# Dealing the routed token rows over the slot columns: ranks of an expert over eight groups of four, half of the experts backwards

## The reference

```python
group_p = softmax(xf @ w_group_router)            # 8 groups
g_w, g_idx = top_k(group_p, 1)
e_logits = (xf @ w_expert_router).reshape(N, 8, 8)
in_group = take_along_axis(e_logits, g_idx)       # the 8 experts of the group
e_w, e_idx = top_k(softmax(in_group), 2)          # two of them
gate = g_w * (e_w / sum(e_w))
expert = g_idx * 8 + e_idx
...                                               # per expert e, for its tokens:
a, b = split(x @ w_up[e], 2);  y = (silu(a) * b) @ w_down[e]
```

## Time and profile before

| | |
|---|---|
| median of 3 runs | 1333.13 us (1330.25 to 1333.38) |
| profiled execution, its own time | 1332.49 us |
| its span | 1330.7 us |
| mean granted clock of TensorE | 0.939 |
| routing, from its first constant to the first pair's up product | 629.2 to 670.3 us |
| pairs, first up product to the end of the last | 670.3 to 1191.2 us |
| busy share of the span | TensorE 85%, VectorE 47%, ScalarE 24%, GpSimd 18% |

### The profile page before, as it was taken

How to read it: one execution, slowest core, us unless ns; L and a number is a source line. 1 busy time by engine, 2 the same in 40 slices (tenths; PEclk the granted TensorE clock), 3 DMA queues, 4 the chain that set the end, 5 groups by cost and what they waited for, 6 DMA issues and landing times. The chain is left out here.

```text
span 1330.7 us, 16742 instructions
## 1 busy us (share of the span) xinstructions
PE 1125.5 (85%) x6261; PEld 733.2 (55%) x6262; DVE 626.4 (47%) x926; ACT 322.8 (24%) x693; POOL 242.6 (18%) x346
## 2 busy tenths in 40 slices
PE   6999899998788876998988888788878777872996
PEld 5888788876767765887432333333333322322885
DVE  5699999984778765232711111111111111125674
ACT  5212211116555534222311111100000000022332
POOL 4000100003676640001111110111111111101120
PEclk9999999999899997998989998998899988895999
DMA  6111111100000106121999999999999999967331
GB/s 209 32 48 33 47 49 48 48 16 1 1 2 2 65 1 214 64 95 47 415 393 427 424 424 413 423 404 399 409 413 406 412 401 401 408 267 270 133 127 64
DMA packets 70170, 281.30 MB, mean 211 GB/s; under 512 B 12570, under 2 KB 38363, under 8 KB 53467
## 3 DMA queue, kind: packets, MB, share of 16 engines
q1 hardware_dynamic: 57120, 258.53, 49.3%
q0 software_dynamic: 9376, 16.80, 3.3%
q10 hardware_dynamic: 3610, 5.11, 1.0%
HBM read 268.08 MB, written 29.62 MB: 224 GB/s over the span
## 5 line engine op out<-in xcount | busy, mean ns | idle before, releaser
L2582 PE MATMUL ps_u<-wup,xgT 128*64 128x512 f32 x1024 | 260.1, 666 | 72.3 <-DMA wup<-in_w_up_dram 71.5
L2582 PEld LDWEIGHTS ps_u<-wup,xgT 128*64 128x64 f32 x1024 | 87.0, 153 | 241.8 <-issue 240.8
L2449 DVE TENSOR_TENSOR hb<-sil,ps_u 128x256 f32<-128x256 f32 x32 | 13.5, 421 | 330.5 <-ACT sil L2343 330.5
L94 PE MATMUL ps_b<-n_hi,wh 128*128 128x512 f32 x384 | 157.7, 411 | 0.6 <-DVE wl L431 0.6
L94 PE MATMUL ps_b<-n_lo,wh 128*128 128x512 f32 x384 | 152.0, 396 | 0.0
L94 PE MATMUL ps_b<-n_hi,wl 128*128 128x512 f32 x384 | 151.8, 395 | 0.0
L2343 ACT ACTIVATE sil<-ps_u 128x256 f32<-128x256 f32 x32 | 12.3, 385 | 312.3 <-PE ps_u L2582 312.3
L94 PE MATMUL ps_y<-wg_hi,hx 128*128 128x512 f32 x256 | 83.4, 403 | 2.5 <-DVE hx L2524 2.5
L94 PEld LDWEIGHTS ps_b<-n_hi,wh 128*128 128x128 f32 x384 | 73.2, 191 | 16.5 <-issue 2.5
L94 PEld LDWEIGHTS ps_b<-n_hi,wl 128*128 128x128 f32 x384 | 73.1, 190 | 16.4
L94 PEld LDWEIGHTS ps_b<-n_lo,wh 128*128 128x128 f32 x384 | 73.3, 191 | 15.0 <-issue 1.0
(11 more groups left out here) (372 smaller groups left out, 1841.8 us busy)
## 6 DMA issues: line engine op xcount, KB each, us to landing
wup<-in_w_up_dram SPq DMA_DIRECT2D x64, 2048.0 KB, 16.7
zT<-in_w_down_dram SPq DMA_DIRECT2D x32, 1024.0 KB, 18.0
convT<-in_w_down_dram SPq DMA_DIRECT2D x32, 1024.0 KB, 17.3
wraw<-in_w_in_dram SPq DMA_DIRECT2D x24, 512.0 KB, 4.3
convT<-y_rows SPq DMA_DIRECT2D x16, 512.0 KB, 4.7
qkvT<-in_x_dram SPq DMA_DIRECT2D x8, 512.0 KB, 8.6
qkvT<-in_w_out_dram SPq DMA_DIRECT2D x8, 512.0 KB, 5.3
xr<-in_x_dram SPq DMA_DIRECT2D x8, 512.0 KB, 3.4
```

Of the source, the lines that this page charges most:

```text
L94: ins = nc.tensor.matmul(ps, lhs[a], rhs[b], start=first and k == 0, stop=last and k == 2)
L2449: nc.vector.tensor_tensor(hb[k][rows], sil[k][rows], ps_u[k][rows, FE:2 * FE], ALU.mult).then_inc(s_h, 1)
L2582: last = nc.tensor.matmul(ps_u[k][HC[c], :], xgT[k][:, j, HC[c]], wup[k][c][:, j, :], start=j == 0, stop=j == NJ - 1)
```

## The change

It has three parts. `iP` becomes one pattern over the 128 partitions: partition 32a + 4b + c (a 0 to 3, b 0 to 7, c 0 to 3) carries the slot value 32a + 8c + b. Consecutive ranks of an expert therefore go to partitions 4 apart, over eight groups of four partitions, and the upper expert now counts up from slot 64. Second, the experts whose place in their group (0 to 7) is 4 or more are filled backwards: `slot` becomes 63 - `slot`. For that the place in the group, `i1` and `i2` before, is kept in one tile `in`, and three instructions of VectorE are added: one that makes `back` (-2 for the experts concerned, else 0) and two that apply it. Third, `iP` takes one instruction of GpSimd in place of two, so the waits for s_iota count one less. Experts p and p + 32 have the same place in their groups, so both of a pair run the same way. Loops, buffers, waits and transfers of the pairs' stage are the same.

```diff
@@ constants and tiles
-t1 = {... "m1", "i1", "m2", "i2", "ex", ...}
-t2 = {n: ... for n in ("ev", "rank", ...)}
+t1 = {... "m1", "m2", "ex", ...}
+t2 = {n: ... for n in ("in", "back", "ev", "rank", ...)}
+            HS = P // 4
@@ vector
-                dve.wait_ge(s_iota, 10)
+                dve.wait_ge(s_iota, 9)
-                first(t8["ing"][:], t1["m1"][:], t8["e1"], t8["c1"], t1["i1"], t8["o1"])
+                first(t8["ing"][:], t1["m1"][:], t8["e1"], t8["c1"], t2["in"][:, :, 0:1], t8["o1"])
-                first(t8["d2"][:], t1["m2"][:], t8["e2"], t8["c2"], t1["i2"], t8["oh"])
+                first(t8["d2"][:], t1["m2"][:], t8["e2"], t8["c2"], t2["in"][:, :, 1:2], t8["oh"])
...
                 tt(ohs[:], oh[:, :, 0, :], oh[:, :, 1, :], ALU.add, "ohs")
+                then(nc.vector.tensor_scalar(t2["back"][:], t2["in"][:], -100.0 + 3.5, -2.0, ALU.is_ge, ALU.mult))
...
                 tt(t2["pair"][:], t2["c"][:], t2["ep"][:], ALU.add)
+                then(nc.vector.scalar_tensor_tensor(t2["b"][:], t2["slot"][:], -0.5 * (C - 1), t2["back"][:], ALU.add, ALU.mult))
+                tt(t2["slot"][:], t2["slot"][:], t2["b"][:], ALU.add)
                 tt(t2["a"][:], t2["up"][:], t2["mn"][:], ALU.mult)
                 tt(t2["slot"][:], t2["slot"][:], t2["a"][:], ALU.add)
@@ gpsimd
-                iota(iP[:, 0:C], [[1, C]], 0, 0)
-                iota(iP[:, C:P], [[-1, C]], P - 1, 0)
+                iota(iP, [[HS, P // HS], [1, 8], [8, HS // 8]], 0, 0)
...
-                pool.wait_ge(s_iota, 9)
+                pool.wait_ge(s_iota, 8)
@@ tensor
-                pe.wait_ge(s_iota, 10)
+                pe.wait_ge(s_iota, 9)
```

More of the change, by code:

```diff
@@ L1811, in hybrid_block_kernel @@
             t8 = {n: sb("r8_" + n, W8, ctx=c6) for n in ("gd", "ge", "eq", "ca", "oh", "ing", "d", "e1", "c1", "o1", "d2", "e2", "c2")}
-            t1 = {n: sb("r1_" + n, [P, NT, 1], ctx=c6) for n in ("gm", "gs", "gw", "gi", "m1", "i1", "m2", "i2", "ex", "dn", "rc")}
-            t2 = {n: sb("r2_" + n, [P, NT, 2], ctx=c6) for n in ("ev", "rank", "m", "slot", "ovk", "pk", "a", "b", "c", "up", "ep", "pair", "mp", "mn")}
+            t1 = {n: sb("r1_" + n, [P, NT, 1], ctx=c6) for n in ("gm", "gs", "gw", "gi", "m1", "m2", "ex", "dn", "rc")}
+            t2 = {n: sb("r2_" + n, [P, NT, 2], ctx=c6) for n in ("in", "back", "ev", "rank", "m", "slot", "ovk", "pk", "a", "b", "c", "up", "ep", "pair", "mp", "mn")}
             big = sb("r_big", [P, NT, NG, 8], ctx=c6)
@@ L1887, in _ @@
                 at["m2"] = done
-                first(t8["d2"][:], t1["m2"][:], t8["e2"], t8["c2"], t1["i2"], t8["oh"])
-                for k, i_k in enumerate(("i1", "i2")):
-                    then(nc.vector.scalar_tensor_tensor(t2["ev"][:, :, k:k + 1], t1["gi"][:], 8.0, t1[i_k][:], ALU.mult, ALU.add))
+                first(t8["d2"][:], t1["m2"][:], t8["e2"], t8["c2"], t2["in"][:, :, 1:2], t8["oh"])
+                for k in range(2):
+                    then(nc.vector.scalar_tensor_tensor(t2["ev"][:, :, k:k + 1], t1["gi"][:], 8.0, t2["in"][:, :, k:k + 1], ALU.mult, ALU.add))
                 then(nc.vector.tensor_scalar(t2["ev"][:], t2["ev"][:], 900.0, None, ALU.add))
@@ L1958, in iota @@
                 def iota(t, pattern, base, mult):
-                    nc.gpsimd.iota(t, pattern, base=base, channel_multiplier=mult, allow_small_or_imprecise_dtypes=True).then_inc(s_iota, 1)
-                iota(i8[:], [[1, 8]], 0, 0)
-                iota(i64[:], [[1, NE]], 0, 0)
-                iota(iP[:, 0:C], [[1, C]], 0, 0)
-                iota(iP[:, C:P], [[-1, C]], P - 1, 0)
-                iota(iN[:], [[1, NIP]], 0, 0)
-                iota(val[:], [[P, NT], [T, 2]], 1, 1)
+                    nc.gpsimd.iota(t[:], pattern, base=base, channel_multiplier=mult, allow_small_or_imprecise_dtypes=True).then_inc(s_iota, 1)
+                iota(i8, [[1, 8]], 0, 0)
+                iota(i64, [[1, NE]], 0, 0)
+                iota(iP, [[HS, P // HS], [1, 8], [8, HS // 8]], 0, 0)
+                iota(iN, [[1, NIP]], 0, 0)
+                iota(val, [[P, NT], [T, 2]], 1, 1)
                 nc.gpsimd.memset(on16[:], 1.0).then_inc(s_iota, 1)
```

## The result

The changed kernel takes 1312.8 us (median of four runs, 1312.5 to 1314.1) against 1332.0 us (four runs of the kernel before). The ratio is 0.9858, with a 95% interval of 0.9841 to 0.9875: 19.2 us faster, where 17.5 were forecast. The forecast of 1315.5 us is 2.7 us too high and its range of 1310 to 1322 holds the result. Measured again beside the experiments on one chip, it was 1314.0 against 1334.1, ratio 0.9853 (0.9836 to 0.9870). The profiled execution took 1312.5 us, span 1310.8.

A forecast was written before the change was run, and what follows sets the result against it. The prediction took the most heavily loaded DMA engine to set the pairs' pace. Rows -18.0 us and routing +0.5 gave -17.5 from the profiled 1332.5, so 1315.0; adjusted to the runs' median, 1315.5 us was forecast, range 1310 to 1322.

The forecast's parts named there:

- split A: Weight and row transfers: each DMA engine moves four neighbouring partitions and the four 32 further on, within one half.
- the working of the prediction: Pairs' stage, 28 gaps: 14.84 us a pair for an engine's weights plus 0.155 us per row of the heaviest engine.
- Split C: Rival, row transfers: groups of four partitions dealt round all 16 engines, without running ahead; 9.9 us more, 1343.5; chance 0.03.
- The rows: -18.0 us: Pairs' stage: the heaviest engine's counted rows fall from 374 to 258, at 0.155 us each, 18.0 us less.
- Running ahead: Pairs' stage: engines work ahead on issued transfers; with the new lead, at most 24 rows or 7.4 us, none runs dry.
- mark for running dry: Pairs' stage: at a lead of 43 rows (pair 8) the 10 us of issued work is passed and the rate drops.
- +0.5 us of the routing: Routing at the start: three VectorE instructions cost 0.63 us, the single iota saves 0.1; sum +0.5 us.
- TensorE's wait was to fall by the gain, to 50 to 55 us: Up products in the pairs' stage: TensorE's wait for wup, 69.8 us before, falls by about the gain.
- Total rate or nothing left: Rival, pairs' stage: total rate is the limit or rows are already even; only routing's half microsecond is left, 1333.7; chance 0.06.
- Pair by pair: Rival, pairs' stage: engines cannot run ahead usefully, each pair costs its own largest share; -12.4 + 0.5, 1321 us; chance 0.11.

The follow-up runs named there:

- no gathered rows: Kernel before with every gather index beyond the bound, so no token row is read, scatters kept; 1299.1 us, ratio 0.9741.
- both halves even: Changed kernel with the two experts swapping slot halves in every second pair, five VectorE instructions added; 1312.4 us, then 1310.9.
- indices later: Changed kernel with twelve more small VectorE instructions ahead of the one-hots, delaying the gathers' indices; 1316.9 us, ratio 0.9865.
- backwards alone: Changed kernel with the earlier partition order of iP put back, half of the experts still filled backwards; 1315.7 us, ratio 0.9867.
- dealing alone: Changed kernel without the three VectorE instructions: ranks dealt over eight groups of four partitions, no expert backwards; 1313.3 us, ratio 0.9863.
- heaped: Kernel before with another iP alone, putting each eight successive ranks on partitions of one engine by split A; 1353.4 us, ratio 1.0150.

## Why the prediction was right, and where its terms were off

**One engine sets the pace, split A.** Shown, by the times; no trace names the engine of a packet. Ten profiles, the rows of the heaviest engine between the up products of pairs 3 and 31, the working of the prediction (28 x 14.84 + rows x 0.155), and what was measured, in us:

| kernel | rows | worked out | measured |
|---|---|---|---|
| no gathered rows | 171 | 442.0 | 440.5 |
| both halves even, twice | 219 | 449.5 | 449.6, 450.0 |
| changed kernel, twice | 236 | 452.1 | 451.6, 451.0 |
| changed kernel, indices later | 236 | 452.1 | 451.1 |
| backwards alone | 242 | 453.0 | 452.1 |
| dealing alone | 256 | 455.2 | 454.1 |
| before | 342 | 468.5 | 469.8 |
| heaped | 440 | 483.7 | 488.8 |

The counts come from the split and the reference's routing, not from the traces. The measured times follow the rows without an exception. Split C, counted in the same way, gives 246 rows for the kernel before and for the heaped one alike and 387 for dealing alone, where 469.8, 488.8 and 454.1 us were measured. Nor is it one slow engine with its own rows: the engine of the last partitions, the heaviest before, has 211 rows with dealing alone and 231 in the changed kernel, and the first of these took longer.

**The rows: -18.0 us.** The mechanism was right, the size a little small. For the part between pairs 3 and 31 the same price gave -16.4, and -18.2 was measured (469.8 to 451.6). The table shows where the rest is: with little imbalance the price of 0.155 us fits within 1.5 us, with more of it the time runs over, by 1.3 us at 342 rows and 5.1 at 440. A straight line through all ten has 0.178 us a row, one through the eight with 171 to 256 rows has 0.157. The price had been taken where all engines are full; what else a run-dry state costs wasn't in it. The packet records of the traces narrow it down. A row's packet takes the same 0.160 us in the stretch of the heaped kernel as in that of the changed one (mean of 3452 each). A 16 KB packet of the weights takes 0.615 us on average in the changed kernel, 0.632 in the kernel before and 0.645 in the heaped one, with medians of 0.611 to 0.614 in all three. The difference is a few long ones: over 0.7 us are 0.2%, 5% and 7% of them, and in the kernel before 0.5% from 720 to 800 us but 11% from 1080 to 1150, when the rate has fallen. Whether they are on the heaviest engine isn't in the record, so the cause stays open.

**Running ahead.** Shown by backwards alone. The new lead of 24 rows empties no engine: the rate is 424 GB/s from pair 3 to pair 31. The prediction's mark for running dry, a lead of 43 rows or 10 us of issued work, is too low: dealing alone has 425 GB/s at 44 rows. In the kernel before, the slices of the earlier trace rows stay below 415 only from 865 us on, where pair 12 makes it 59 rows, and not from pair 8. The new lead was far enough below either mark.

**+0.5 us of the routing.** The added instructions do reach the gathers. That they reach the end is likely, as twelve of them went with a first product 3.6 us later and a median 2.9 us longer, but not clear of the scatter. From the routing's first `iota` to the first gather's issue the traces have 28.49 us before, 28.66 with dealing alone (the new `iota`, none of the three instructions), 29.15 with backwards alone (the three instructions, the old `iota`), 29.28 in both profiles of the change, 30.33 in both of the halves with five instructions more, and 31.81 with twelve more. So an added instruction costs 0.21 us each time, and the three cost 0.66, as worked out (0.63). The `iota` was mis-sized, and beyond its bounds of -0.13 to +0.03: it was to save 0.1, and the one after it starts 0.39 us later, where it was 0.26.

```profile
630.24 0.43 POOL L1963 IOTA iP<- 128x128 f32 x1
630.63 0.20 POOL L1963 IOTA iN<- 128x65 f32 x1
```

Together the term was +0.8 and not +0.5, up to the gathers. Yet the first product came 0.9 us sooner after the routing's start. From the first gather's issue to the first product the profiles have 12.6 us before, and 10.9, 10.6, 12.2, 11.5, 10.8, 11.8, 12.0 and 12.0 in those of the changed kernel (twice), dealing alone, backwards alone, the halves (twice), heaped and late. That scatter doesn't go by how even the rows are, so I can't say that the change shortens this part; it is larger than the term. What differs lies ahead of the point where all engines meet (L1803): GpSimd's first copy behind it, of `gi_x`, starts 10.6 us after the gather's issue before, 8.9 in the changed kernel's first profile and 10.0 in the late one, and the same 2.0 us later comes the product in all three.

**TensorE's wait was to fall by the gain, to 50 to 55 us.** Off. Between the same products, the group of the up product, as in the earlier trace rows, in the changed kernel's first profile and then in its second:

```profile
L2585 PE MATMUL ps_u<-wup,xgT 128*64 128x512 f32 x898 | 219.3, 644 | 62.5 <-DMA wup<-in_w_up_dram 62.5
```

```profile
L2585 PE MATMUL ps_u<-wup,xgT 128*64 128x512 f32 x896 | 228.4, 666 | 55.0 <-DMA wup<-in_w_up_dram 55.0
```

The wait fell from 69.8 to 62.5 in the one and to 55.0 in the other; what the one has less in products (219.3 against 228.4 us) it has more in waiting. Over the whole span the granted clock was 0.947 in the first and 0.936 in the second, of the upper of the two levels, 2.4 GHz. The pace didn't care: 451.6 and 451.0 us. The wait is what is left over by a TensorE that isn't the bound, so its change is a poor measure of a gain.

**The number.** The forecast was 17.5 us, and 19.2 were measured. The rows gave 1.8 us more in the stretch than their price had, the routing's term took 0.3 more than its own; that makes 19.0, and the last 0.2 us are less than the runs scatter.

**The rivals.** Total rate or nothing left: out by the heaped kernel and by the rate. Pair by pair: out by backwards alone. Split C: out by the heaped kernel and by dealing alone. The Trainium skill's rule on the engine of a partition (DMA: Bandwidth & Descriptors, The descriptor swizzle) thus fits the indirect transfers of this case: the times worked out with it are within 1.5 us of the measured ones in all kernels but the heaped one. Its figure of about 358 GB/s for a core's HBM (SBUF — State Buffer, A bandwidth-pool intuition that's wrong) doesn't bind here: 424 GB/s through 450 us.

## What to carry to other kernels

A DMA share near 1 on average doesn't say that all engines are needed: look whether the rate falls in the course of a stage whose work stays alike, and count, per engine, the rows of indirect transfers whose empty slots move no row. What counts is the total per engine over as many steps as the issued work reaches ahead, so it is enough to change the direction of filling every few steps (here every four pairs). An uneven load that falls on the same engines in each step is the one that costs.

## What the runs showed of the hardware that was not expected

Heaping the rows made the kernel 20.8 us slower where 16.4 were worked out. One more row on the heaviest engine cost 0.157 us (the line through the eight profiles with 171 to 256 rows) while the rate was high, and some 0.19 ((488.8 - 469.8) / 98) from the kernel before to the heaped one. The packet of a row took 0.159 us (median) in either. An index beyond the bound is not quite nothing: with no gathered rows, 2048 packets of 4096 bytes are gone from the rows' queue and 2048 more of 4 bytes are there, of 0.009 us each (median of all of that size). The `iota` of three levels and 128 columns took 0.43 us, where two plain ones of 64 took 0.31 together. And between the issue of the first gather and the first up product, 10.6 to 12.6 us passed in the nine profiles with gathers, with no order by the evenness of the rows.
